# Hybrid recurrent decoder step on one core: head norms from one row a head, spread by TensorE, with gates and query-key norms done beside the even input projection

## What is computed

```python
def rmsnorm(x, w):
    y = x * lax.rsqrt(jnp.mean(x * x, axis=-1, keepdims=True) + EPS)
    return y * w
def l2norm(x):
    return x * lax.rsqrt(jnp.sum(x * x, axis=-1, keepdims=True) + EPS)
# even mixer (DeltaNet + SSD), after projection, causal conv and silu
q = l2norm(q.reshape(bsz, L, 4, 128)) * (128 ** -0.5)
k = l2norm(k.reshape(bsz, L, 4, 128))
beta = sigmoid(dn_b);  g = -exp(dn_a_log) * softplus(dn_a + dn_dt_bias)      # the gates
o_dn, s = gated_delta_rule(q, k, v, beta, g, s0)
o_dn = rmsnorm(o_dn, dn_norm_w) * silu(dn_gate)             # 4 heads of 128
y = rmsnorm((y + ssm_d * xs) * silu(ssm_z), ssm_norm_w)     # 2 groups of 256
# odd mixer (GLA)
o = rmsnorm(o, norm_w) * silu(og)                           # 4 heads of 256
# retrieval, a token at a time
act = gelu(u_tab[expert] . t) * gate;  y = sum(act * v_tab[expert])
```

## Time and profile before

| | us |
|---|---|
| median of three executions | 3635.71 |
| lowest, highest | 3620.84, 3642.60 |
| the profiled execution's own time | 3628.32 |
| its span, first to last instruction | 3626.3 |
| prologue, up to the first dot product on DVE (gather 0) | 410.8 |
| PE, DVE, ACT, POOL busy | 2918.4, 2447.7, 1211.3, 1229.8 |
| moved by DMA | 1225.40 MB |

### The profile page before, as it was taken

The page is one execution under the profiler, slowest core; times in us unless marked ns, Lnnn a source line. Parts: engine busy times, 40 slices in busy tenths (PEclk is TensorE's granted clock), DMA queues, the critical chain, the costliest instruction groups (busy, mean ns, idle before and its releaser), DMA issues.

```text
span 3626.3 us, 31512 instructions
## 1 busy us (share of the span) xinstructions
PE 2918.4 (80%) x9692; PEld 1666.1 (46%) x9692; DVE 2447.7 (67%) x4978; ACT 1211.3 (33%) x3532; POOL 1229.8 (34%) x1094
## 2 busy tenths in 40 slices
PE   7678498688888788797887898787788787788775
PEld 6567365455555256454532256454454242222222
DVE  3463787886876897667667587666667878545444
ACT  3211244433333333423233242432223343333333
POOL 0010123444433333433333333334334444334332
PEclk9889799899899899979999799889799889999998
DMA  4103488799989898979999799989899899999996
GB/s 157 59 1 132 188 330 329 302 379 386 409 357 418 336 387 356 383 280 377 418 419 420 302 377 378 355 303 417 336 416 419 337 381 417 386 375 373 420 420 281
DMA packets 183659, 1225.40 MB, mean 338 GB/s; under 512 B 21185, under 2 KB 21585, under 8 KB 48194
## 3 DMA queue, kind: packets, MB, share of 16 engines
q0 software_dynamic: 153088, 1115.26, 76.7%
q1 hardware_dynamic: 30402, 108.12, 7.9%
HBM read 1211.46 MB, written 11.84 MB: 337 GB/s over the span
## 4 chain that ended last, share of the span: by engine, by line
PE 33%; DMA 29%; DVE 26%; issue 4%; ACT 4%; DVEq 3%; POOL 1%; SPq 0%; ACTq 0%; POOLq 0%
PE ps L493 32%; DMA ring<-in_uv,picked 28%; DVE ring L1961 8%; DVE otok L1920 2%; ACT scratch L957 1%; DVEq L1732 1%; DVE scratch L1736 1%; DVE scratch L1738 1%; DVE scratch L1742 1%; DVE scratch L1767 1%; DVE scratch L1762 1%; ACT diag L957 1%; DVE ids L1769 1%; POOL ring L478 1%; ACT gated L957 1%
## 5 line engine op out<-in xcount | busy, mean ns | idle before, releaser
L493 PE MATMUL ps<-ring,diag 128*128 128x512 f32 (+1 forms) x3380 | 1760.5, 652 | 421.5 <-ACT diag L957 419.8
L478 POOL DMA_INDIRECT ring<-in_uv,picked x1024 | 1163.3, 1136 | 1988.2 <-PE ps L493 1394.6
L1961 DVE SCALAR_TENSOR_TENSOR ring<-ring,htok 128x1024 f32<-128x1024 f32 x1024 | 1248.2, 1227 | 629.0 <-DMA ring<-in_uv,picked 622.1
L493 PEld LDWEIGHTS ps<-ring,diag 128*128 128x128 f32 (+1 forms) x3380 | 628.8, 201 | 1303.1 <-ACT diag L957 761.1
L957 ACT ACTIVATE act_v<-pre 128x1 f32<-128x1 f32 x1040 | 210.5, 202 | 1815.7 <-DVE ring L1961 1814.4
L493 PE MATMUL ps<-hT,wring 128*128 128x256 f32 (+1 forms) x3200 | 750.7, 390 | 54.2 <-DVE hT L1269 27.3
L493 PEld LDWEIGHTS ps<-hT,wring 128*128 128x128 f32 x3200 | 621.2, 195 | 229.7 <-issue 92.5
L957 ACT ACTIVATE diag<-masks,gated 128x128 f32<-128x128 f32 x829 | 332.9, 402 | 35.4 <-PE ps L493 8.4
L957 ACT ACTIVATE gated<-act_v,gates 128x1 f32<-128x1 f32 x1024 | 301.8, 295 | 33.4
L493 PE MATMUL ps<-scratch 128*128 128x128 f32 (+3 forms) x1236 | 199.5, 306 | 60.1 <-ACT scratch L957 13.5
L1920 DVE SCALAR_TENSOR_TENSOR otok<-ring,gated,otok 128x1024 f32<-128x1024 f32 x189 | 244.2, 1292 | 0.0
(11 more groups left out here) (300 smaller groups left out, 1683.5 us busy)
## 6 DMA issues: line engine op xcount, KB each, us to landing
wring<-in_weights SPq DMA_DIRECT2D x200, 512.0 KB, 7.8
ring<-in_uv,picked POOLq DMA_INDIRECT x1024, 11.4
scratch<-in_keys POOLq DMA_DIRECT2D x4, 1024.0 KB, 11.2
scratch<-in_s_gla POOLq DMA_DIRECT2D x4, 1024.0 KB, 12.1
out_o_gla<-scratch POOLq DMA_DIRECT2D x4, 1024.0 KB, 12.5
xT<-in_xT SPq DMA_DIRECT2D x1, 2080.0 KB
scratch<-in_s_dn POOLq DMA_DIRECT2D x1, 2048.0 KB, 9.5
scratch<-in_s_ssm POOLq DMA_DIRECT2D x1, 2048.0 KB, 15.1
```

The source lines that it names most:

```text
L478: pool.indirect_dma_start(out=ring[:, g % RING, :], out_offset=None, in_=io["uv"][L], in_offset=bass.IndirectOffsetOnAxis(ap=index, axis=0 ...
L493: return pe.matmul(out, lhsT, rhs, start=start, stop=stop)
L1961: stt(x, x, 1.0, h, MUL, MUL, accum_out=pre[:, g % SMALL:g % SMALL + 1]).then_inc(sem("dotted"), 1)
```

## The change

1. Sums of squares no longer stand on all partitions. `head_sums` uses as weights 8 columns of a one-hot matrix (`oneh`), so that the sum of head h lands in row h of one 8-row result in PSUM; ACT takes one root of 8 x n elements into `root_rows` (scale and offset by row from `eps`), DVE one reciprocal of it (`inverse`), and `head_rows` spreads each row over 128 partitions with a matmul whose weights are one column of the identity (8 rows). DVE multiplies from PSUM.
2. The gates and the query-key norm of the even mixer move into `gemm("even_in")` (`beside_even_in`): gates' matmuls after blocks 3, 4 and 5, sums after block 14, rows after block 18; ACT's part at blocks 8, 10 and 14, DVE's at blocks 6, 10, 14 and 18. The 8 sample tokens of pair 1 get a small norm of their own around the start of the scan.
3. The slots of pair 1 move: the even scan from 56 to 50, sample tokens from 130 to 124, mix from 166 to 160, `even_out` from 173 to 171, `query0` from 190 to 188. The odd mixers' `odd_out` moves back by 2 slots (8 after O_MIX becomes 10), `query1` too. Three starts of choices move by 2.

The diff, cut to its core:

```diff
-E_NORM, E_IN, E_GATE, E_L2, E_SCAN, E_SCAN_LEN = 0, 8, 46, 52, 56, 37
-E_SAMPLE, E_MIX, E_OUT, E_QUERY = 130, 166, 173, 190
...
 SKEW = 8
 O_NORM, O_IN, O_GK, O_SCAN, O_SCAN_LEN = 0, 13, 62, 70, 18
 O_SAMPLE = 106
...
-O_MIX, O_OUT, O_QUERY = (107, 148), (115, 156), (137, 178)
+O_MIX, O_OUT, O_QUERY = (107, 148), (117, 158), (139, 180)
...
+            def head_sums(out, squares, heads, first=True, final=True):
+                for i, h in enumerate(heads):
+                    last = mm(out, oneh[:, NS_TOK * h:NS_TOK * h + NS_TOK], squares(i),
+                              first and i == 0, final and i == len(heads) - 1)
+                if final:
+                    last.then_inc(sem("sums_ready"), 1)
+
+            def head_rows(outs, n):
+                for h, out in enumerate(outs):
+                    last = mm(out, ident[0:NS_TOK, h:h + 1].to_broadcast([NS_TOK, P]), root_rows[0:NS_TOK, 0:n])
+                last.then_inc(sem("rows_ready"), 1)
+
+            def even_gates(p, i):
+                if p and i == 0:
+                    pe.wait_ge(sem("htok_ready"), 2)
+                rows = NS_TOK if i == 2 else P
+                for c in range(KD):
+                    last = mm(ps[0:rows, 4, 16 * i:16 * i + 16], hT[:, c, i * P:i * P + rows], small_w[:, c, :],
+                              c == 0, c == KD - 1)
+                if i == 1 + p:
+                    last.then_inc(sem("gates_mm"), 1)
+
+            def beside_even_in(p, j):
+                if j in range(3, 5 + p):
+                    even_gates(p, j - 3)
+                if j == 14:
+                    pe.wait_ge(sem("sq_ready"), SQ_L2[p])
+                    head_sums(ps[0:NS_TOK, 5, 0:256], lambda b: sq_qk[:, b, :], range(8))
+                if j == 18:
+                    pe.wait_ge(sem("gates_read"), p + 1)
+                    pe.wait_ge(sem("inverse"), L2[p])
+                    head_rows([ps[:, 4 + b // 2, (b % 2) * 256:(b % 2) * 256 + 256] for b in range(8)], 256)
...
                     last.then_inc(sem("gemm_done"), 1)
+                    if name == "even_in":
+                        beside_even_in(p, j)
...
-                pe.wait_ge(sem("l2_done"), 2 * (n // 2) + 2)
+                pe.wait_ge(sem("l2_done"), n // 2 + 1)
+                pe.wait_ge(sem("conv_silu"), 5 + 6 * (n // 2))
+                pe.wait_ge(sem("gemm_free"), FIRST_BLOCK["even_in", n // 2] + BLOCKS["even_in"])
...
                 if p:
-                    pe.wait_ge(sem("htok_ready"), 2)
-                tiles = (0, 1) if p == 0 else (0, 1, 2)
-                for i in tiles:
-                    rows = NS_TOK if i == 2 else P
-                    for c in range(KD):
-                        if c % 4 == 0:
-                            yield even_slot(p, E_GATE + 2 * i + c // 4)
-                        last = mm(ps[0:rows, 4, 16 * i:16 * i + 16], hT[:, c, i * P:i * P + rows], small_w[:, c, :],
-                                  c == 0, c == KD - 1)
-                last.then_inc(sem("gates_mm"), 1)
-                for r in range(2):
-                    yield even_slot(p, E_L2 + 2 * r)
-                    pe.wait_ge(sem("gates_read"), p + 1)
-                    pe.wait_ge(sem("sq_ready"), 4 * p + r + 1)
-                    if r:
-                        pe.wait_ge(sem("roots_ready"), 4 * p + r)
-                    for b in range(4):
-                        last = mm(ps[:, 4 + b, 0:n], ones, sq8[:, 4 * r + b, 0:n])
-                    last.then_inc(sem("sums_ready"), 1)
+                    yield even_slot(p, E_SCAN)
+                    pe.wait_ge(sem("sq_ready"), SQ_SAMPLE)
+                    head_sums(ps[0:NS_TOK, 7, 0:NS_TOK], lambda b: sample_sq[:, b, :], range(8))
                 if p == 0:
                     side_by_side(scan_even)
...
-                        yield from scan_even(2 * p + i)
-                if p:
+                    yield from scan_even(2)
+                    yield even_slot(p, E_SCAN + E_SCAN_LEN)
+                    pe.wait_ge(sem("inverse"), SAMPLE_L2)
+                    head_rows([ps[:, 7, 64 + NS_TOK * h:64 + NS_TOK * h + NS_TOK] for h in range(8)], NS_TOK)
+                    yield from scan_even(3)
                     yield from sample_even()
-                yield even_slot(p, E_MIX)
+                yield even_slot(p, E_MIX + 3)
                 pe.wait_ge(sem("mixed"), p + 1)
-                pe.wait_ge(sem("sq_ready"), 4 * p + 3)
-                for b in range(4):
-                    last = mm(ps[:, 4 + b, 0:n], ones, sq8[:, b, 0:n])
-                last.then_inc(sem("sums_ready"), 1)
-                yield even_slot(p, E_MIX + 1)
-                pe.wait_ge(sem("sq_ready"), 4 * p + 4)
-                for b in range(4):
-                    last = mm(ps[:, 2 + b // 2, 0:n], ones, sq8[:, 4 + b, 0:n], b % 2 == 0, b % 2 == 1)
-                last.then_inc(sem("sums_ready"), 1)
+                pe.wait_ge(sem("sq_ready"), SQ_MIX[p] - 1)
+                head_sums(ps[0:NS_TOK, 4, 0:n], lambda b: sq8[:, b, 0:n], range(4), final=False)
+                yield even_slot(p, E_MIX + 4)
+                pe.wait_ge(sem("sq_ready"), SQ_MIX[p])
+                head_sums(ps[0:NS_TOK, 4, 0:n], lambda b: sq8[:, 4 + b, 0:n], (4, 4, 5, 5), first=False)
+                yield even_slot(p, E_MIX + 8)
+                pe.wait_ge(sem("inverse"), MIX[p])
+                head_rows([ps[:, b, 0:n] for b in (4, 5, 6, 7, 2, 3)], n)
                 yield from gemm("even_out", p, even_slot, E_OUT, None)
...
                 pe.wait_ge(sem("mixed"), 3 + p)
-                pe.wait_ge(sem("sq_ready"), 9 + p)
-                for b in range(8):
-                    if b == 4:
-                        yield odd_slot(p, O_MIX[p] + 1)
-                    last = mm(ps[:, 4 + b // 2, 0:n], ones, o_sq[:, b, 0:n], b % 2 == 0, b % 2 == 1)
-                last.then_inc(sem("sums_ready"), 1)
+                pe.wait_ge(sem("sq_ready"), SQ_ODD[p])
+                head_sums(ps[0:NS_TOK, 4, 0:n], lambda b: o_sq[:, b, 0:n], (0, 0, 1, 1, 2, 2, 3, 3))
+                yield odd_slot(p, O_MIX[p] + 6)
+                pe.wait_ge(sem("inverse"), ODD_MIX[p])
+                head_rows([ps[:, 4 + h, 0:n] for h in range(4)], n)
                 yield from gemm("odd_out", p, odd_slot, O_OUT[p], None)
                 yield from norm(3, p)
                 yield from gemm("query1", p, odd_slot, O_QUERY[p], 3)
...
-            def roots(count, out, in_, scale, e):
+            def roots(count, in_, scale, bias):
                 act.wait_ge(sem("sums_ready"), count)
...
+                    if j == 10:
+                        act.wait_ge(sem("conv_silu"), 5 * p + 2)
+                        if p:
+                            act.wait_ge(sem("score_mm"), score_no(1))
+                        f(sq_qk, conv[:, 0:8, 0:256], ACT.Square).then_inc(sem("sq_ready"), 1)
+                    if j == 14:
+                        roots(L2[p], ps[R8, 5, 0:256], eps[R8, 3:4], eps[R8, 4:5])
                 yield even_slot(p, E_IN + done_off("even_in", 27) + 2)
                 act.wait_ge(sem("gemm_free"), FIRST_BLOCK["even_in", p] + 28)
...
                     f(x, x, ACT.Silu).then_inc(sem("conv_silu"), 1)
-                yield even_slot(p, E_L2 - 1)
-                act.wait_ge(sem("conv_silu"), 5 + 6 * p)
...
-                yield even_slot(p, E_L2 + 1)
-                roots(4 * p + 1, sq8[:, 0:4, 0:n], ps[:, 4:8, 0:n], float(P), 1)
-                yield even_slot(p, E_L2 + 2)
-                act.wait_ge(sem("gates_abs"), p + 1)
-                f(g_abs[:, r], g_abs[:, r], ACT.Exp, scale=-1.0).then_inc(sem("gates_exp"), 1)
-                if p == 0:
-                    f(neg_a, a_log[:, :], ACT.Exp)
-                act.wait_ge(sem("gates_exp"), p + 1)
-                f(g_abs[:, r], g_abs[:, r], ACT.Ln, bias=eps[:, 2:3])
-                f(beta[:, r], g_raw[:, r, 12:16], ACT.Sigmoid).then_inc(sem("gates_act"), 1)
-                yield even_slot(p, E_L2 + 3)
-                roots(4 * p + 2, sq8[:, 4:8, 0:n], ps[:, 4:8, 0:n], 1.0, 0)
+                    act.wait_ge(sem("conv_silu"), 11)
+                    f(sample_sq, conv[:, 0:8, 256:264], ACT.Square).then_inc(sem("sq_ready"), 1)
+                    yield even_slot(p, E_SCAN + 2)
+                    roots(SAMPLE_L2, ps[R8, 7, 0:NS_TOK], eps[R8, 3:4], eps[R8, 4:5])
                 if p == 0:
                     side_by_side(scan_even)
...
                 act.wait_ge(sem("ssm_gated"), p + 1)
                 f(sq8[:, 4:8, 0:n], hT[:, 4:8, 0:n], ACT.Square).then_inc(sem("sq_ready"), 1)
-                roots(4 * p + 3, sq8[:, 0:4, 0:n], ps[:, 4:8, 0:n], 1.0 / P, 0)
-                yield even_slot(p, E_MIX + 2)
-                roots(4 * p + 4, sq8[:, 4:6, 0:n], ps[:, 2:4, 0:n], 1.0 / 256, 0)
+                yield even_slot(p, E_MIX + 4)
+                roots(MIX[p], ps[R8, 4, 0:n], eps[R8, 5:6], eps[R8, 0:1])
                 yield from norm(1, p)
```

(80 more changed lines are left out.)

47 lines of the change are left out of this document (30 added, 17 removed).

## The result

The changed kernel takes 3601.0 us in the median (3574.8 to 3618.3, four runs), the kernel before 3639.2 us beside it on the same chip: ratio 0.9887, 95% interval 0.9838 to 0.9936. By the ratio that is 41 us less, by the medians 38; the prediction had 46 (3590, range 3566 to 3618).

What follows compares the result with a forecast made beforehand. The prediction saw a serial chain in the prologue, then DMA transfers, with PE binding the loop beside pair 1's `even_in`. Prologue 23.9 plus loop 34.8 minus added work 12.8 gave 45.9 us off 3635.7: 3590 us, range 3566 to 3618.

Steps and rivals of the forecast that it cites:

- Prologue: Before the gather loop: scan 16.2 us earlier, 2.2 from a higher clock, output norm 5.5; together 23.9 us gained.
- 16 x 0.43 = 6.9 us: Prologue projection: PE time added by the query-key norm's 8 sums and 8 rows, each at full price.
- Output norm: Prologue, second square to `even_out`: smaller root, reciprocal and products gain 5.5 us, bounds 3.0 to 7.4.
- ACT's burst of three loads: Prologue gates: three table loads and four small activations, about 5 us of ACT, hidden beside the projection without stalling PE.
- 15.8 + 8 - 12.8: Pair 1: query-key norm dip filled (15.8 us), even output norm dip (8), less work added to the PE-bound stretch (12.8).
- 8 of 8.8 us: Even output norm of pair 1: share of the DMA idle time at 995 to 1015 counted as gained.
- Odd norms: Odd layers of both pairs: one reciprocal instead of two, 10 slots instead of 8, gaining 5.5 us each.
- 5.5 of 6.2 us: Odd norm of pair 1: share of the DMA idle time at 2595 to 2615 counted as gained.
- (a): Rival: bursts beside the bound projection cost 24 us, smaller dips go by half; 26 us gained, about 3610; chance 0.17.
- (b): Rival: all bounds come out well, reciprocals and PE's idle time alone caused the dips; 54.6 us gained, 3581; chance 0.12.
- (c): Rival: pair 1's scan waits for another condition, so the 15.8 us stay; 30 us gained, 3606; chance 0.11.
- (d): Rival: a PE wait inside pair 1's projection drops its clock to 1.2 GHz; slower, 3663 with 70% so; chance 0.05.

Runs made afterwards that it cites:

- full_rows: Changed kernel with the query-key norm's rows spread by calls of 128 rows (120 zeros) instead of 8; ratio to the kernel before 0.9863.
- late_p1: Changed kernel with pair 1's gates, sums and rows moved from blocks 3 to 18 of its projection to blocks 20 to 27; ratio to the kernel before 0.9818.
- wide_sample: Changed kernel with the sample units' sum of the values formed with 128 columns of weights instead of 8; ratio to the kernel before 0.9844.
- full_spread: Changed kernel with the samples' rows in the two sample units spread by calls of 128 rows instead of 8; ratio to the kernel before 0.9854.
- beside_only: Changed kernel with the old output norms, keeping only gates and query-key norm beside the even projections; ratio to the kernel before 0.9952.
- all_and_scan: late_all with the odd scans' state update also made by calls of 128 rows instead of 32; 3541.2 us, ratio to the kernel before 0.9712.
- late_all: Changed kernel with the edits of late_p1, full_rows, wide_sample and full_spread together; 3567.8 us, ratio to the kernel before 0.9818.
- late_full: Changed kernel with the edits of late_p1 and full_rows together; ratio to the kernel before 0.9858.

## Why the prediction was right, and where its terms were off

**Sum.** 45.9 us forecast, 41 and 39 measured (ratios 0.9887 and 0.9892 of about 3637). Right in sign and size, with terms that came out smaller nearly everywhere. Two small slips of the sum go against each other: 149.8 - 133.5 is 16.3, not 16.2, and the middle of 268.4 and 272.8 is 270.6, which makes the output norm 5.2 and not 5.5.

**Prologue: 23.9 forecast, 18.1 measured** (mean of the six traces with the same pair 0, by their first dot product: 21.7, 16.8, 18.7, 15.9, 18.3 and 16.9). The chain was read rightly: the scan follows the projection with a wait of 0.57 us, its first 34 records in 4.03 us (5.91 before; 1.9 gained for 2.2). The term that was too small is "16 x 0.43 = 6.9 us": it priced the calls and not the clock behind them, worth 2.0 us. So the scan starts 12.8 us sooner in the mean of the six, for 16.2; the other 1.4 us lie ahead of the rows, where the traces differ among themselves. `full_rows`, without the fall, starts it at 134.3, my 133.5 within a microsecond; its rows took 3.62 us with 128 rows, 3.71 with 8. Output norm, from the first square to `even_out`: 21.5 us before, 14.7 in the trace after, 6.8 gained for 5.5. But the six traces have 14.7 to 18.2 us, 4.6 gained in the mean; three of them at 18.2, above the 12 to 15 us of my signs, one at 17.3 (`late_p1`, with the rows at the low clock). All lie inside my bounds of 3.0 to 7.4. ACT's burst of three loads hid as costed, with 1.28 us loads and the next activation 1.29 us behind a load's start (62.82 and 64.11); of the drain that the Trainium skill's page "ScalarE: Activation LUTs" states (about 1380 ns) this trace shows nothing either.

**Pair 1: 11.0 forecast (15.8 + 8 - 12.8), 5.3 measured** (12 to 213 in four traces with the changed code there: 8.0, 4.2, and 6.8 and 2.3 in `wide_sample` and `full_spread`). The price was right in size: 12.6 us by gather 37 (130.4 for 117.8) for 12.8, paid in PE's time as argued, shown by taking the calls away and by doubling them; 2.0 us of it are the lost clock, which the sum did not have. The wait is gone too: no dip ahead of the scan, none at the even output norm. Up to gather 128 the four traces gain 0.9 us in the mean, for 15.8 - 12.8 = 3.0. What failed is the step from a filled dip to a gained microsecond at the even output norm, "8 of 8.8 us": 128 to 213 gives 4.5 us in the mean of the four (2 to 7), and in the eight other traces with the small output norm between 5.2 gained and 4.6 lost. The stretch varies with PE's clock beside the scans and the sample tokens. That the clock took the rest is argued from its rows, not shown; why `beside_only` loses 8 us more than before between gathers 128 and 213 stays open too.

**Odd norms: 11.0 forecast, 8.9 and 9.6 measured.** Their own stretches give 5.9 + 9.2 = 15.1 us and 4.9 + 10.8 = 15.7 us in the two traces, but the projections moved back by 2 slots return 2.9 + 3.3 = 6.2 of them in the 20 gathers behind. That cost was in no term of the sum. The 5.5 of 6.2 us that I counted as filled for pair 1 are filled behind the norm, but of the 11.1 us that DMA was idle around it 8.9 are left, at a wait ahead of the norm that the sum did not look at; the stretch is shorter by 9.2 all the same. The three parts are 18.1 + 5.3 + 8.9 = 32.3 us of the 38 that the medians show; the other 6 us lie elsewhere, where single traces differ by more than that, so how closely a sum of parts meets the medians is partly luck.

**Rivals.** (a), given back, holds for pair 1 alone and there by half. (b) no. (c) no: with the norm out of the way the scan itself waits for nothing over 1 us; the one long wait of PE ahead of it, 7.3 us at 602.6, is for a gather's diagonal matrix, with DMA at 1.02. (d), the clock: its mechanism was wrong (the change put no wait of PE there that let the clock fall), and a weaker form is true: the added calls of 8 rows do it, with PE busy throughout, at a cost of 2.0 us behind eight calls in the prologue and again in pair 1, 3.4 us more where they stand twice. I had priced these calls by rows that are "as slow as full ones"; that holds for their own duration and misses what comes behind them.

## What to carry to other kernels

Take one root and one reciprocal of an 8-row tile and let TensorE spread it: that is worth it even where the norm stays in its place. Moving work beside a loop pays where the loop has the engine free, so look which engine bounds each stretch; one stretch later the same calls cost nothing here, though the whole kernel did not keep that lead for certain. Fill the array's rows: pad a matmul of 8 rows with zeros to 128 where its duration stays the same. And measure a stretch far enough: a gain at a norm can come back as a cost at the projection behind it, and a cost of PE can show at VectorE one gather after the stretch has ended.

## What the runs showed of the hardware

- Matmuls that fill 8 of the 128 rows are followed by a lower granted clock although PE is busy throughout: 0.69 behind 8 calls of 8 x 256 (all seven traces that have them in the prologue lose 1.7 us of clock there), and 0.54 to 0.83 as the mean of a sample unit (PE busy in 43.3 of 45.8 us at 0.54); with 128 rows it is 1.00 behind the calls in all four traces, and 0.94 to 1.00 in the three sample units. For 32 rows only the runs speak (`all_and_scan`), not a stretch. More columns of weights (128 for 8) did not help. The Trainium skill's page "TensorE: Matmul & The Clock Gate", section "Part 1: The HAM clock gate", ties the lower level to a TensorE that has been idle; here it fell without any idle time in the row, and the measurement decides.
- By and large the runs of higher mean clock are the shorter ones (3573.7 at 0.922, 3620.9 at 0.911). Whether calls of few rows make the spread between executions is not shown: it is 47 us in the changed kernel's twelve runs, 19 in `full_spread`'s six and 23 in `all_and_scan`'s six, but 37 in `late_all`'s six and 20 in those of `late_full`, which keeps 8 rows in its sample units.
- Eight calls of 256 columns took 3.62 us with 128 rows and 3.71 us with 8: filling the rows costs PE no time.
